# Two-block transformer kernel: gate units ahead of the attention, second half by token halves and single heads, 28 gather buffers

## The chip, the cores and the metric

The kernel runs on one core of one Trainium2 chip. The metric is the device time of one execution in microseconds (us); the kernel before takes 1839.51 us, the median of 3 runs (1837.49 to 1839.92). All data are 32-bit floats.

## The reference

`x` is 256 tokens of 1024 numbers. The first block (a convolution branch, a windowed attention, a mixture of experts) is not touched by the change, except for the order of two loads at its very start. The second block is, cut to what matters:

```python
h = modulate(rmsnorm(x, norm_mix_g), sh1, sc1)
q, k, v, z_hy, gates = split(h @ w_in)
attn = gqa_blocks(q, k, v)            # 8 heads; q and k normed and rotated; plus the context's k, v
hy = hyena(z_hy, ...)                 # short convolution, two long ones (as products of spectra)
g_attn, g_hy = split(gates)           # 1024 columns each
merged = (sigmoid(g_attn) * (attn @ w_attn_out)
          + sigmoid(g_hy) * (hy @ w_hy_out))
x = x + g1 * (merged @ w_out)
xt = modulate(rmsnorm(x, norm_ffn_g), sh2, sc2)
# peer(), in chunks of 128 tokens, 8 heads:
q = xt @ wq                           # 8 heads x 2 halves x 128
s1, s2 = q[.., 0] @ keys1.T, q[.., 1] @ keys2.T   # 128 keys each
v1, i1 = top_k(s1, 16); v2, i2 = top_k(s2, 16)
best, pos = top_k(v1[:, None] + v2[None, :], 16)  # of the 256 sums
eidx = 128 * i1[pos // 16] + i2[pos % 16]         # a row of 16384
a = einsum('chkd,cd->chk', u_tab[eidx], xt)
wgt = gelu(a) * softmax(best)
x = x + g2 * einsum('chk,chkd->cd', wgt, v_tab[eidx])
out = rmsnorm(x, final_norm_g)
```

Each token takes 8 x 16 = 128 rows of 4 KB from each of two tables. That is 512 gathers of 128 rows (512 KB each): 256 of table u, 256 of table v.

## The kernel before

It is written out by hand, engine by engine, with semaphores; program order on each engine is the order below. Feature-major tiles hold 256 tokens in columns (`actT`: 8 chunks of 128 features), token-major ones 128 tokens in the partitions (t = 0, 1). Weights come in pieces of 2 MB through the six slots of `ring`, in the order of `pieces2`; SyncE (SP) reloads a slot when the PSUM bank that last used it is full. A matrix product fills one of the eight PSUM banks; `last.then_inc(bank_full[b])` hands it to VectorE (DVE) or ScalarE (ACT), which empties it (`copy_out`, `half_out`). Nearly all matrix products are recorded on one line, L405 (`mm`), transposes on L413, L926, L942 and others.

The second block on TensorE (PE), in order:

1. the projections q and kv (token-major), then `hy0` to `hy2` (6 units of 16 products 128x256);
2. transposes of q and k; `k2_ready` is set by DVE when it has rotated q and k, done the short convolution and copied the keys;
3. the attention, 16 units of scores, softmax, transposes and products with v, with the parts of the hyena convolutions between them; it runs hand in hand with DVE and ACT;
4. `merge`: eight gate units (16 products 128x256 each) and eight output units (8 products each) in turn, each pair over all 256 tokens; `bmerged` at the end;
5. the transposes of the keys (L926), the output projections `out_unit_rows` of (t, n) = (0,0), (0,1), (1,0), the transposes of the normed tokens of t = 0, the projection (1,1);
6. `queries` (32 products 128x128 each, one per piece pq0 to pq3 and t), `key_scores` (t, g) for two heads each, and `tokens_back`, which leaves the tokens in PSUM banks 0 to 3 for the dots.

DVE then does for each group j of two heads (j = 0 to 7, t = j // 4) `picks_of(j)`: the top 16 of four lists of 128, the top 16 of two lists of 256 sums, and the rows' numbers; the last step sets `rowid_ready`. `dots_of(j)` multiplies each of the group's 32 gathered rows of u with the tokens (L2093, one instruction per row). `weigh(j)` needs the exponentials of ACT. PE sums the rows of v (`sum_rows`, L999: two products 128x512 with a diagonal matrix per row, which ACT makes on L1453); in the last two groups every other row is summed by DVE (L2124).

GpSimd (POOL) issues the 512 gathers, one after the other (L1150), group by group in the order of `TURNS`: u0, u1, v0, u2, v1, u3 and so on to v7. Gather n goes to buffer n % 24 and waits until the row of gather n - 24 has been read. The buffers are the ring's slots 1 to 4, 0 and part of 5; a buffer's first use waits for the piece of weights that held it (`slot_reader`), five first uses take spare tiles instead. The order of DVE is picks 0, picks 1, dots 0, weigh 0, then for j = 1 to 7: dots j, weigh j, picks j + 1. On ACT the copies of all key scores stand ahead of the first exponentials.

## Time and profile before

| | |
|---|---|
| median of 3 runs | 1839.51 us (1837.49 to 1839.92) |
| the profiled execution | 1844.83 us; its span 1842.8 us |
| PE, DVE, ACT, POOL busy | 81%, 48%, 16%, 27% of the span |
| chain that ended last | PE 73%, issue 9%, POOL 6%, DMA 5%, DVE 3%, an unknown queue 3% |
| HBM read | 563.5 MB, of it 268.8 MB on the queue of the gathers |

All stages below are in time from the start of the span: the first block ends near 750 us, the second block's dense part runs from there to about 1043 us, when the first gather is issued, and the gathers and sums run to the end. PE is busy nearly all the time up to 1043 us and about six tenths of it afterwards. "Issue" and "remote" as what ended an idle time mean that the profile shows nothing that the engine waited for, or a queue that it doesn't know.

### The profile page before, as it was taken

Reading aid. Unit: us, or ns where it says so; the run is one execution under the profiler, and the core shown is the slowest. Engines: PE = TensorE matmul, PEld = TensorE weight load, DVE = VectorE, ACT = ScalarE, POOL = GpSimd, SP = SyncE. Lnnn points to the kernel's source line nnn. Section 1 sums busy time; section 2 is a strip of 40 time slices with the busy share of each in tenths; the row PEclk is TensorE's granted clock in tenths of the full one; section 3 lists DMA queues with packets and bytes.
Section 4 is the critical chain, followed back from the end, with each engine's and each line's share of the span. In section 5 each row is a group of like instructions: output and inputs, shape, how many; then the busy total and the mean of one; then the engine's idle time right before and its main releaser. Section 6 shows DMA issues by size and latency. Waiting matters only on the chain.

```text
span 1842.8 us, 17400 instructions
## 1 busy us (share of the span) xinstructions
PE 1497.4 (81%) x6106; PEld 826.1 (45%) x6106; DVE 889.1 (48%) x1991; ACT 303.8 (16%) x634; POOL 501.4 (27%) x540
## 2 busy tenths in 40 slices
PE   7999989999999999889999862765858584848376
PEld 6866564443434434575786762322323231313122
DVE  3986143322223232465302774484646556564844
ACT  3113222111101111214201103020202020211001
POOL 3000000000000000000000255657574757575764
PEclk9999989999999999999999976787878786878798
DMA  9649458999999999630134488979897989898996
GB/s 320 246 143 375 163 246 342 427 428 428 429 429 428 429 429 415 223 137 1 58 114 145 148 311 315 371 273 396 303 411 293 397 303 384 301 392 301 388 374 258
DMA packets 135272, 565.35 MB, mean 307 GB/s; under 512 B 11497, under 2 KB 17430, under 8 KB 122732
## 3 DMA queue, kind: packets, MB, share of 16 engines
q1 hardware_dynamic: 60588, 295.66, 40.2%
q0 software_dynamic: 74416, 268.84, 38.3%
q8 instruction: 32, 0.52, 0.1%
q14 instruction: 28, 0.23, 0.0%
q10 hardware_dynamic: 208, 0.09, 0.0%
HBM read 563.49 MB, written 1.06 MB: 306 GB/s over the span
## 4 chain that ended last, share of the span: by engine, by line
PE 73%; issue 9%; POOL 6%; DMA 5%; DVE 3%; another core or an unknown queue 3%; ACT 1%; SPq 0%; DVEq 0%; ACTq 0%
PE psum L405 52%; PE psum L999 20%; POOL ring L1150 6%; DMA ring<-in_ada_w_dram 2%; DMA ring<-in_peer_v_dram,attnT 2%; DMA ring<-in_peer_u_dram,attnT 1%; DVE scratch L2093 1%; DMA arena<-in_hf_w_dram 1%; PE psum L413 0%; PE psum L785 0%; PE psum L791 0%; SPq L1013 0%; PE psum L860 0%; DVE ring L1961 0%
## 5 line engine op out<-in xcount | busy, mean ns | idle before, releaser
L999 PE MATMUL psum<-ring,arena 128*128 128x512 f32 x904 | 440.8, 639 | 268.8 <-DMA ring<-in_peer_v_dram,attnT 140.3
L1150 POOL DMA_INDIRECT ring<-in_peer_u_dram,attnT x251 | 236.1, 941 | 1190.4 <-DVE attnT L2067 1070.7
L999 PEld LDWEIGHTS psum<-ring,arena 128*128 128x128 f32 x904 | 182.0, 204 | 527.1 <-issue 395.7
L2093 DVE CUSTOM_DVE_ANT_0 scratch<-ring,psum 128x1024 f32<-128x1024 f32 x251 | 303.8, 1221 | 86.0 <-DMA ring<-in_peer_u_dram,attnT 57.8
L405 PE MATMUL psum<-ring,arena 128*64 128x512 f32 (+1 forms) x1552 | 343.8, 594 | 1.4 <-DVE arena L1822 1.4
L405 PE MATMUL psum<-actT,ring 128*128 128x256 f32 (+1 forms) x1424 | 269.2, 349 | 28.7 <-issue 26.9
L1150 POOL DMA_INDIRECT ring<-in_peer_v_dram,attnT x256 | 246.6, 963 | 129.3 <-issue 82.6
L405 PEld LDWEIGHTS psum<-actT,ring 128*128 128x128 f32 x1424 | 238.9, 197 | 58.0 <-issue 34.8
L405 PEld LDWEIGHTS psum<-ring,arena 128*64 128x64 f32 (+1 forms) x1552 | 110.5, 137 | 219.2 <-issue 205.8
L1864 DVE TENSOR_TENSOR arena<-arena,psum 128x512 f32<-128x512 f32 x16 | 16.9, 1058 | 203.9 <-PE psum L405 203.9
L1453 ACT ACTIVATE arena<-ident,attnT 128x128 f32<-128x128 f32 x226 | 72.8, 390 | 170.5 <-remote 67.8
L405 PEld LDWEIGHTS psum<-arena,scratch 128*128 128x128 f32 x544 | 63.3, 192 | 13.3 <-issue 13.3
L405 PE MATMUL psum<-arena,scratch 128*128 128x128 f32 x544 | 67.8, 278 | 0.0
L405 PE MATMUL psum<-tok,arena 128*128 128x512 f32 x128 | 59.2, 605 | 0.0
L2124 DVE SCALAR_TENSOR_TENSOR scratch<-ring,attnT,scratch 128x1024 f32<-128x1024 f32 x29 | 37.2, 1284 | 43.3 <-DMA ring<-in_peer_v_dram,attnT 33.2
L405 PE MATMUL psum<-ring,tok 128*128 128x512 f32 x128 | 56.0, 595 | 1.6 <-DVE tok L1691 1.6
L1190 ACT ACTIVATE arena<-psum 128x512 f32<-128x512 f32 x38 | 22.7, 597 | 197.4 <-PE psum L405 155.0
L1888 DVE TENSOR_TENSOR resid<-resid,psum 128x512 f32<-128x512 f32 x64 | 44.0, 688 | 13.8 <-PE psum L405 13.8
L1437 ACT ACT_TABLE_LOAD x7 | 9.0, 1283 | 250.7 <-DVE attnT L2080 250.6
L2025 DVE MAX8 qT<-arena 128x8 f32<-128x128 f32 x64 | 17.1, 288 | 66.8 <-remote 47.4
L1577 DVE SCALAR_TENSOR_TENSOR arena<-arena,colsB 128x256 f32<-128x256 f32 x120 | 47.7, 477 | 0.0
L1882 DVE COPY tok<-psum 128x512 f32<-128x512 f32 x16 | 11.1, 692 | 72.9 <-PE psum L405 72.9
(380 smaller groups left out, 1196.1 us busy)
## 6 DMA issues: line engine op xcount, KB each, us to landing
ring<-in_w_gate_dram SPq DMA_DIRECT2D x32, 2048.0 KB, 12.1
ring<-in_w_up_dram SPq DMA_DIRECT2D x32, 2048.0 KB, 16.5
ring<-in_w_down_dram SPq DMA_DIRECT2D x32, 2048.0 KB, 14.3
ring<-in_w_in_dram SPq DMA_DIRECT2D x15, 2048.0 KB, 14.9
ring<-in_ada_w_dram SPq DMA_DIRECT2D x12, 2048.0 KB, 11.7
ring<-in_w_out_dram SPq DMA_DIRECT2D x4, 2048.0 KB, 8.8
ring<-in_peer_wq_dram SPq DMA_DIRECT2D x4, 2048.0 KB, 10.5
ring<-in_w_attn_out_dram SPq DMA_DIRECT2D x2, 2048.0 KB, 8.9
```

Source lines behind the costliest of these rows:

```text
L405: return nc.tensor.matmul(o, lhsT, rhs, start=(k == 0), stop=(k == n - 1))
L999: last = nc.tensor.matmul(psum[:, 4 + 2 * t + n, :], diag[:, i, :], row_buf(b, use)[:, n * 512:(n + 1) * 512], start=first, stop=final)
L1150: pool.indirect_dma_start(out=row_buf(b, use), out_offset=None, in_=tab, in_offset=bass.IndirectOffsetOnAxis(ap=rowid[:, j // 4, k:k + 1], ...
L1190: last(nc.scalar.activation(dst, full(act, name)[:, 0:w], func, **kw), name)
L1453: nc.scalar.activation(diag[:, i, :], ident[:, :], ACT.Identity, scale=gates[:, j // 4, k:k + 1]).then_inc(ev("diag_ready"), 1)
L1577: V.scalar_tensor_tensor(yT[:, c, :], vpad[:, c, j:j + T], w, yT[:, c, :], ALU.mult, ALU.add).then_inc(ev("tap"), 1)
L1864: V.tensor_tensor(hperm, silu.rearrange("p (q k) -> p q k", k=4), psum[0:BOTH, 4, :].rearrange("p (q k) -> p q k", k=4), ALU.mult).then_in ...
L1882: V.tensor_copy(yrow[:, 512:1024], psum[0:BOTH, 6, :]).then_inc(ev("y_ready1"), 1)
L1888: V.tensor_tensor(r, r, psum[:, MIX_BANK[n, t], :], ALU.add).then_inc(ev("mixed"), 1)
L2025: v_pair(V.max(vals[:, 8 * r:8 * r + 8], src))
L2093: V.tensor_tensor_reduce(dotjunk[:, i % 2, :], row_buf(b, use), x, 1.0, 0.0, ALU.mult, ALU.add, dots[:, t, k:k + 1]).then_inc(ev("dotted"), 1)
L2124: V.scalar_tensor_tensor(acc, row_buf(b, use), w, acc, ALU.mult, ALU.add).then_inc(ev("added"), 1)
```

## The change

The weights get another order, with a slot for each piece given by hand. All eight gate units stand ahead of the attention: the four of the first branch behind the hyena projections, the four of the second behind the transposes of q and k. ACT keeps their sigmoids, the first four in `mergedT`, the second four over `actT`. After the attention the output units are done by token halves (`mixed_half`, 16 products 128x128), the merge by token halves (`merge_half`), and the norm, queries and key scores of t = 0 start while t = 1 is unfinished. The queries and key scores of group 0, and its picks, are done by single heads; `rowid_ready` is set once for each. There are 28 row buffers, filled by a table `ROW_ORDER` up to gather 53 and after that by which was read the longest ago; eight dots of group 0 are done between the steps of t = 1. The second output gate row, the keys and the final gain have other places in memory. At the start, the piece `wg` is issued behind four small loads. Some semaphores are shared by name.

```diff
-ROWBUFS = 24
+ROWBUFS = 28
...
+        rowbufs = [dft[:, :, :, :].rearrange("p a t c -> p (a t c)"), idft[:, :, :].rearrange("p a t -> p (a t)")]
+        rowbufs += [ring[:, 3, r * D:(r + 1) * D] for r in range(4)] + [ring[:, 4, r * D:(r + 1) * D] for r in range(4)]
+        rowbufs += [tok2[:, 0, :], tok2[:, 1, :]]
+        rowbufs += [ring[:, s_, r * D:(r + 1) * D] for s_ in (2, 5, 1, 0) for r in range(4)]
...
+        ROW_ORDER = [*range(10), *range(4), 10, 11, *range(4, 8), *range(12, 20), *range(8, 12), *range(0, 6), *range(20, 24), *range(6, 10), *range(12, 16), *range(24, 28)]
...
-            pe.wait_ge(ev("qk2_ready"), 1)
+            gate_units2(0)
+            pe.wait_ge(ev("proj_ready"), 1)
...
+            gate_units2(1, (4, 5, 6, 7))
             emptied(pe, "qT0")
             emptied(pe, "qT1")
-            pe.wait_ge(ev("k2_ready"), 1)
+            pe.wait_ge(ev("proj_ready"), 3)
...
-            merge(place2, "b", [(attnT, tuple(f"pw{i}" for i in range(4))), (hyoT, ())])
+            def mixed_half(br, t, u):
+
+                wo = ring[:, place2[f"o{br}"][0], :].rearrange("p (k n) -> p k n", k=KC)
+                b = bank(f"bo{br}{t}{u}")
+                for c in range(4):
+                    m = (4 * u + c) * P
+                    for k in range(KC):
+                        last = mm(psum[:, b, c * P:(c + 1) * P], wo[:, k, m:m + P], (attnT, hyoT)[br][:, k, t * P:(t + 1) * P], k, KC)
+                last.then_inc(bank_full[b], 1)
...
+            room_reader = {2: "bo011", 6: "bo111", 10: "bx11", 12: "pq01", 16: "pq11", 20: "pq21", 24: "pq31"}
...
+                    if table == "u" and (i == 0 or (j == 0 and i == PTOP)):
+                        pool.wait_ge(ev("rowid_ready"), j + 2 if j else 1 + (i > 0))
+                    if use == 1 and b in room_reader:
+                        full(pool, room_reader[b])
+                    if use > 1:
+                        reader, count = row_reader(before_)
                         pool.wait_ge(ev(reader), count)
...
-            picks_of(0)
+            best_of(0, (0,), "0a")
+            rows_of_table(0, (0,))
+            merge_half(1, 1, 1)
+            best_of(0, (1,), "0b")
+            rows_of_table(0, (1,))
+            shift_of(0)
+            mix_in(1, 0)
+            dots_of(0, range(0, 4), 1)
+            mix_in(1, 1)
+            dots_of(0, range(4, 5), 1)
+            pn_rows(1)
+            dots_of(0, range(5, 8), 1)
+            half_out("pn", 1, modsc[:, 2, :], mod[:, 24:32, 0])
             picks_of(1)
-            dots_of(0)
+            dots_of(0, range(8, GROUP))
```

The order on PE from the hyena projections (the first row) to the first scores, before:

```order
L405 MATMUL psum<-actT,ring 128x256 x96
L839 MATMUL psum<-ident,arena 128x128 x8
L844 MATMUL psum<-ident,arena 128x128 x2
L405 MATMUL psum<-kdup,qT 128x512 x4
L883 MATMUL psum<-ident,arena 128x128 x8
```

and in the changed program:

```order
L404 MATMUL psum<-actT,ring 128x256 x160
L822 MATMUL psum<-ident,arena 128x128 x8
L827 MATMUL psum<-ident,arena 128x128 x2
L404 MATMUL psum<-actT,ring 128x256 x64
L404 MATMUL psum<-kdup,qT 128x512 x4
L867 MATMUL psum<-ident,arena 128x128 x8
```

64 products of the gates now stand ahead of the transposes of q and k, and 64 between these and the scores (`kdup,qT`).

PE again, from the last of the eight pairs of gate and output units to the second group's scores (`ring,tok` are the output projections, `actT,ring` 128x128 the queries, `spec,arena` the key scores), before:

```order
L405 MATMUL psum<-actT,ring 128x256 x16
L405 MATMUL psum<-arena,ring 128x256 x8
L926 MATMUL psum<-ident,ring 128x128 x16
L405 MATMUL psum<-ring,tok 128x512 x24
L413 MATMUL psum<-ident,scratch 128x128 x8
L405 MATMUL psum<-ring,tok 128x512 x8
L405 MATMUL psum<-actT,ring 128x128 x32
L413 MATMUL psum<-ident,scratch 128x128 x8
L405 MATMUL psum<-spec,arena 128x128 x4
L405 MATMUL psum<-actT,ring 128x128 x32
```

and in the changed program, from the third and fourth half of the output units on:

```order
L404 MATMUL psum<-arena,ring 128x128 x32
L404 MATMUL psum<-attnT,ring 128x128 x16
L404 MATMUL psum<-ring,tok 128x512 x16
L404 MATMUL psum<-attnT,ring 128x128 x16
L932 MATMUL psum<-ident,arena 128x128 x16
L412 MATMUL psum<-ident,scratch 128x128 x8
L404 MATMUL psum<-arena,ring 128x128 x16
L404 MATMUL psum<-actT,ring 128x128 x16
L944 MATMUL psum<-ident,actT 128x128 x8
L404 MATMUL psum<-spec,arena 128x128 x2
L404 MATMUL psum<-actT,ring 128x128 x16
L404 MATMUL psum<-arena,ring 128x128 x16
```

Two of the four output projections, three of the four halves of t = 1 and half of the first queries are ahead of the first key scores; the other two projections come later.

DVE, from the end of the second head's picks to the second group's (L2009 and L2010 add an output projection, L2105 is a dot, L2015 and L2016 the norm, L1524 the modulation), in the changed program; before, L2003 to L1524 of t = 1 stood ahead of all picks, and the dots behind the second group's:

```order
L2092 TENSOR_TENSOR attnT<-kdup 128x32
L2009 TENSOR_TENSOR scratch<-spec,psum 128x512
L2010 TENSOR_TENSOR resid<-resid,scratch 128x512
L2105 ISA scratch,attnT<-dft,psum 128x1024
L2105 ISA attnT 128x1
L2105 ISA scratch,attnT<-idft,psum 128x1024
...
L2009 TENSOR_TENSOR scratch<-spec,psum 128x512
L2010 TENSOR_TENSOR resid<-resid,scratch 128x512
L2105 ISA scratch,attnT<-ring,psum 128x1024
...
L2015 RECIPROCAL st<-st 128x1
L2016 TENSOR_SCALAR scratch<-resid,st 128x1024
```

The steps that free t = 1 for PE's later queries now stand behind the picks of both heads and between eight dots.

## Rows read from the trace of the kernel before

**Rows 1.** Windows: busy time per engine, granted clock, DMA share.
```profile
core 0: us, PE busy (x) PEld busy (x) DVE busy (x) ACT busy (x) POOL busy (x), PEclk, DMA share, GB/s
900.00:1000.00 100.00, 100.00 (x455) 83.77 (x454) 12.22 (x18) 9.25 (x15) 0.00 (x0) 1.00 0.34 118
...
1100.00:1150.00 50.00, 13.82 (x94) 13.23 (x94) 23.96 (x45) 17.87 (x44) 29.13 (x31) 0.60 0.83 323
```

**Rows 2.** Timeline of PE, around the attention: start, length, line, idle before.
```profile
774.86 41.60 PE L405 MATMUL psum<-actT,ring 128*128 128x256 f32 x192
...
822.68 3.69 PE L405 MATMUL psum<-kdup,qT 64*128 64x512 f32 x8 [5.13 <-DVE st L1944]
...
905.11 7.07 PE L405 MATMUL psum<-actT,ring 128*128 128x256 f32 x32
912.01 3.62 PE L405 MATMUL psum<-attnT,ring 128*128 128x256 f32 x16
```

**Rows 3.** Timeline of PE: projections, queries, the last key scores.
```profile
989.75 20.87 PE L405 MATMUL psum<-ring,tok 128*128 128x512 f32 x48
...
1018.20 7.31 PE L405 MATMUL psum<-actT,ring 128*128 128x128 f32 x64
...
1037.64 12.56 PE L405 MATMUL psum<-actT,ring 128*128 128x128 f32 x111
...
1108.23 0.37 PE L405 MATMUL psum<-actT,ring 128*128 128x128 f32 x1 [1.74 <-issue]
...
1119.76 4.63 PE L405 MATMUL psum<-spec,arena 128*128 128x128 f32 x40
```

**Rows 4.** Timeline of DVE: picks, dots and waits.
```profile
1028.76 0.49 DVE L2025 MAX8 qT<-arena 128x8 f32<-128x128 f32 x2 [0.91 <-ACT arena L1190]
...
1042.87 0.18 DVE L2067 CAST attnT<-attnT 128x32 int32<-128x32 f32 x1
...
1058.18 1.22 DVE L2093 CUSTOM_DVE_ANT_0 scratch<-ring,psum 128x1024 f32<-128x1024 f32 x1
...
1128.24 0.19 DVE L2104 TENSOR_REDUCE st<-attnT 128x2 f32<-128x32 f32 x1 [23.20 <-ACT attnT L1437]
...
1183.01 0.15 DVE L2098 COPY st<-epscol 128x1 f32<-128x1 f32 x1 [2.37 <-remote]
...
1293.36 0.76 DVE L2040 TENSOR_TENSOR spec<-qT 128x256 f32<-128x256 f32 x2 [3.90 <-remote]
```

**Rows 5.** Timeline of POOL: gathers 0, 1, 21, 41, 96 and 175.
```profile
1043.33 1.03 POOL L1150 DMA_INDIRECT ring<-in_peer_u_dram,attnT  x1 [1028.49 <-DVE attnT L2067]
1044.67 0.97 POOL L1150 DMA_INDIRECT ring<-in_peer_u_dram,attnT  x1 [0.30 <-issue]
...
1084.07 0.94 POOL L1150 DMA_INDIRECT ring<-in_peer_u_dram,attnT  x1 [10.55 <-PE psum L405]
...
1120.20 0.94 POOL L1150 DMA_INDIRECT ring<-in_peer_u_dram,attnT  x1 [11.54 <-PE psum L405]
...
1209.21 0.94 POOL L1150 DMA_INDIRECT ring<-in_peer_u_dram,attnT  x1 [11.74 <-DVE attnT L2067]
...
1325.57 0.94 POOL L1150 DMA_INDIRECT ring<-in_peer_u_dram,attnT  x1 [3.13 <-PE psum L999]
```

**Rows 6.** Windows within the gathers, and one whole period.
```profile
1285.00:1290.00 5.00, 1.52 (x2) 0.49 (x2) 1.02 (x5) 0.00 (x0) 1.89 (x3) 0.70 1.03 409
...
1295.00:1300.00 5.00, 4.63 (x6) 1.95 (x6) 4.59 (x22) 0.00 (x0) 2.81 (x3) 0.50 0.48 143
...
1325.00:1330.00 5.00, 5.00 (x13) 2.09 (x11) 4.85 (x9) 2.66 (x8) 3.52 (x4) 1.00 0.92 311
...
1304.07:1400.76 96.69, 65.10 (x138) 27.43 (x137) 56.10 (x133) 13.14 (x36) 60.12 (x64) 0.82 0.91 347
```

**Rows 7.** The page's DMA queues, one row.
```profile
q8 instruction: 32, 0.52, 0.1%
```

**Rows 8.** Timeline of PE at the start of the kernel.
```profile
20.81 0.31 PE L475 MATMUL psum<-ident,kdup 100*128 100x100 f32 x1 [1.15 <-DMA arena<-in_hf_w_dram]
```

More of the change, by code:

```diff
@@ L1 @@
 from contextlib import ExitStack
+import collections
 import itertools
@@ L917, in _ @@
             hy_back(1, 1)
[L918 to L922 removed]
+            def mixed_half(br, t, u):
[5 more added lines that the diff above has]
+                        last = mm(psum[:, b, c * P:(c + 1) * P], wo[:, k, m:m + P], (attnT, hyoT)[br][:, k, t * P:(t + 1) * P], k, KC)
+                last.then_inc(bank_full[b], 1)
+            landed(place2, "o0")
+            for i in range(4):
+                emptied(pe, f"pw{i}")
+            mixed_half(0, 0, 0)
+            mixed_half(0, 0, 1)
+            landed(place2, "o1")
+            pe.wait_ge(ev("hy_ready"), 1)
+            mixed_half(1, 0, 0)
+            mixed_half(1, 0, 1)
+            mixed_half(0, 1, 0)
+            pe.wait_ge(ev("bmerged"), 1)
+            out_unit_rows(place2, "b", 0, 0)
+            out_unit_rows(place2, "b", 0, 1)
+            mixed_half(0, 1, 1)
+            pe.wait_ge(ev("keys_in"), 32)
+            kp = arena1[:, 0:2048].rearrange("p (c d) -> p c d", d=P)
             for g in range(4):
@@ L1359, in _ @@
                 last(nc.scalar.activation(hpad[:, j % 2, :, 1:T + 1], ps, ACT.Copy), f"hy{j // 2}{j % 2}")
+            for i in range(4):
+                copy_out(f"bg0{i}", pair(mergedT, i), func=ACT.Sigmoid)
             for g in range(2):
-                copy_out(f"qT{g}", qT[:, 2 * g:2 * g + 2, :].rearrange("p c t -> p (c t)"))
+                copy_out(f"qT{g}", pair(qT, g))
+            full(act, "bg13")
+            for i in range(4):
+                copy_out(f"bg1{i}", pair(actT, i), func=ACT.Sigmoid)
             def exp_unit(u):
@@ L1376, in hy_spectrum @@
             def hy_spectrum(o, part):
-                if o == 0 and part == 0:
-                    act.wait_ge(ev("y_ready1"), n_iter)
                 for f in range(NT):
@@ L1996, in _, with merge_half @@
             hy_gate(1, 1)
-            merge("b")
+            def merge_half(br, t, u):
+                cs, ts = slice(4 * u, 4 * u + 4), slice(t * P, (t + 1) * P)
+                dst = mergedT[:, cs, ts]
+                ps = full(dve, f"bo{br}{t}{u}").rearrange("p (c t) -> p c t", c=4)
+                if br == 0:
+                    last(V.tensor_tensor(dst, dst, ps, ALU.mult), f"bo{br}{t}{u}")
+                else:
+                    m = mtmp["b"][:, u, :].rearrange("p (c t) -> p c t", c=4)
+                    last(V.tensor_tensor(m, actT[:, cs, ts], ps, ALU.mult), f"bo{br}{t}{u}")
+                    v(V.tensor_tensor(dst, dst, m, ALU.add), "bmerged" if u else None)
+            for br in range(2):
+                for i in range(4):
+                    emptied(dve, f"bg{br}{i}")
+            for br in range(2):
+                for u in range(2):
+                    merge_half(br, 0, u)
+            merge_half(0, 1, 0)
             dve.wait_ge(ev("g1_in"), 16)
```

336 lines of the change are left out of this document (147 added, 189 removed).

## Prediction, made before the changed kernel ran

> **What bounds the kernel now.** I read the windows first: busy time of each engine and DMA share. Ahead of the first gather TensorE is at 100 us of 100 between 900 and 1000 with DMA share 0.34, so there the end is set by PE's products [rows 1]; within the gathers PE is at 13.8 of 50 us in one stretch [rows 1] and at 65 of 96.7 us in a whole period, at DMA share 0.91 [rows 6], so there the transfers and the waits between them set it. The timelines of PE, DVE and POOL then give the steps. PE's row of the attention is preceded by 5.13 us of waiting for DVE [rows 2]. Pairs of a gate unit (7.07) and an output unit (3.62) follow [rows 2]; then projections, 20.87 for three, and queries of t = 0 [rows 3]. DVE's picks start at 1028.76 and its last cast is at 1042.87 [rows 4]; the first gather starts at 1043.33, and the next stands 1.34 later, 0.97 busy and 0.30 between [rows 5]. From then on both ends pull: POOL waits 10.55 and 11.54 us for PE's late queries to free weights' slots [rows 5], while PE itself stands at "issue" (1.74 before one product) and DVE waits 23.20 for ACT's exponentials, which stand behind all copies of the key scores [rows 3, 4]. The third group's u gathers start at 1209.21, after 11.74 of waiting for row numbers [rows 5]. After that the kernel is periodic: 64 gathers (one u and one v group) in 96.69 us [rows 6].
>
> **Where the steady period goes.** A gather is 512 KB; at 409 GB/s, the rate in the stretch at DMA share 1.03 [rows 6], it takes 1.28 us, so 64 take 82 us. The other 15 are two waits. DVE's next picks crawl while the DMA engines are full and get on only when these drain: share 0.48 at 1295 to 1300, with a step of the picks at 1293.36 after 3.90 us of "remote" [rows 4, 6]. And in the u part POOL waits 3.13 us for a buffer that PE has to empty [rows 5], through which DMA keeps going at a share of 0.92 [rows 6], a loss of (1.03 - 0.92) x 5 = 0.6 us in that window and about 1.2 us over the whole wait. My reading of the crawl, on PE and DVE alike, is that their own instructions arrive late: the queue of instructions moved 0.52 MB in 32 packets, 16 KB each [rows 7], through the engines that the gathers fill.
>
> The Trainium skill, "Runtime: NRT & Kernel Launch", section "Instruction fetch mechanics", says that each sequencer fetches 16 KiB blocks by its own DMA queue and that the cost of crossing into a new one is mostly hidden. The packets' size agrees with [rows 7]; "hidden" does not agree with the waits of 1.74 and 3.90 us in [rows 3, 4], if these are such crossings. By the page's rule PE wouldn't be starved; that is rival B below.
>
> **The change, part by part.** The profiled execution has a span of 1842.8 and took 1844.8; the median is 5.3 below that. I sum on the span and carry the difference over.
>
> *Start.* PE waits 1.15 us for a small load at 20.81 [rows 8]; with `wg` behind the small loads this goes, but wg's own product may be late: between -2 (worse) and +1.15. I take +1.
>
> *Gates first.* Eight units of 6.91 (the hyena row has six in 41.60, so 6.93 [rows 2]) move from behind to ahead of the attention: 55.4 us, nothing saved in PE. What they cover: the 5.13 us wait for DVE [rows 2] lies under the second four. But ACT now does four sigmoids between PE's last gate unit and the attention, which bounds this from 0 to the old 5.13; I take a new wait of about the same lag, 4 us, less 2 to 3 hidden. The attention shifts by +52.5 (822.7 to 875.2) and ends near 957.8; the gates are then missing behind it.
>
> *From the attention to the first head's scores.* PE, in order: five output halves of 3.6 (a whole unit, 3.62, is 8 products of 256 columns; a half, 16 products of 128 columns, costs like half a query row of 7.31 [rows 3]: 3.6) = 18; two projections of 6.95 (20.87 / 3 [rows 3]) = 13.9; one half, 3.6; 16 transposes of the keys and 8 of the tokens, 1.9 and 1.0 (at the queries' 7.31 / 64 = 0.114 each [rows 3]); one half, 3.6; half the queries, 3.6; tokens back 1.0, the same way; two scores and their copies, 1.8 by my estimate from short steps of 0.2 to 0.9 [rows 4]. Sum 48.4, so the first picks start near 957.8 + 48 = 1006, against 1028.76 [rows 4]: 23 earlier. The halves have half as many columns each, so double the weight loads; these lie under the products as in [rows 1], where loads take 83.8 us of a full 100.
>
> *Picks of one head.* Both heads took 1042.87 - 1028.76 = 14.1 us [rows 4]. One head is between 7.1 (all by elements) and 14.3 (all fixed cost); the rows are short instructions (0.49 for one list of 128), so nearer to half: 8.7. First gather at 1014.5, 29 us ahead of 1043.33.
>
> *What the second head and t = 1 pay.* `merge_half(1,1,1)` on DVE now stands behind the first head's picks, and `mix_in` of t = 1 behind both heads' with eight dots in between; behind them PE's projections of t = 1, the norm, the transposes and PE's queries of t = 1 wait. I get the projections at 1016 to 1030, the queries of t = 1 at 1042.5, 5 us later than 1037.64 [rows 3]. That order is a price: 5 us of the 29.
>
> *The slots of weights.* POOL's first 28 rows have buffers that come free early or by dots (ten free tiles, then the eight early dots). From gather 28 on it waits for products of PE again, as at 1084.07 and 1120.20 [rows 5], and then for the dots of group 1. So the 29 us are worth only what PE's last queries and DVE's second dots give.
>
> *PE's last queries.* From 1037.64 to the last scores' end at 1124.4 [rows 3] are 86.8 us, for some 51 us of products; 36 are waits at "issue". The gathers now start 29 us earlier and PE's queries 5 later, so PE has about 51 us of work from 1042.5, and is done at 1093.5 if never starved, or at 1093.5 + 36 = 1129.5 if starved as before. POOL is held up from 1041 to 1058 by slots, during which DMA isn't full; some 40 to 45 us of the work see full DMA. With the old ratio (36 lost on some 62 us) these lose 23 to 26. Then ACT's exponentials and DVE: dots of group 1 start near 1120 (between 1098 and 1133), against 1130 (the 23.20 wait ended at 1128.24 [rows 4]).
>
> *To the third group.* Dots of group 1 started near 1130.3, after the small steps behind 1128.24, and their end is 1183.01 [rows 4]: 52.7 us where 32 instructions of 1.14 (1.22 long [rows 4], overlapping by 0.08) are 36.8; from their end to u2 it was 26.2 [rows 4, 5]. So u2 is 63 to 79 us behind the start of the dots. I take 63: 36 gathers left after the dots begin are 46 us of transfer, and behind them about 17 us of drain and picks; the 16 us of starving fell into the old, later queue of gathers. u2 at 1183 against 1209.21: 26 gained, of the 29.
>
> *28 buffers.* Six periods follow. With four more buffers the 3.13 us wait [rows 5] goes. It costs DMA 1.2 us each time: 6 x 1.2 = 7 to 8. Bounds: 0, as picks still end some 10 us after the drain whatever POOL does, and 6 x 3.3 = 20, if all of each wait counts.
>
> Sum: 1 + 26 + 8 = 35. 1839.5 - 35 = **1804**; by the span, 1808.
>
> **Rivals.**
> *A, the above*: with u2 between 1175 and 1195 and the buffers at 0 to 12, 1790 to 1818.
> *B, PE isn't starved in the first groups.* Its waits have shares of ACT's and DVE's emptying in them, and single heads break those up. Dots of group 1 start at 1098, u2 at 1161, 48 earlier; with 6 x 2 us of the buffers and the start, about 60: 1779. It speaks against this that the 1.74 wait has no releaser in the profile [rows 3].
> *C, the change doesn't do what it says*: the early rows are fetched and then stand. All starving remains, the last queries end at 1129.5, group 1's dots start at 1130, and the gathers from 60 on wait for these as before. Left are fewer rows to move behind the dots, 63 to 70 instead of 79, and the buffers: 15 to 23, so about 1820. For it: the waits for PE's slots ended the same [rows 5].
> *D, slower.* With POOL never waiting for a buffer, the DMA engines stay full through each u group, and the block of DVE's instructions that now comes in during a 3 us gap falls into the dots, as in group 1: 16 us there. The place is each of the six later periods, the price up to 9 us each (16, less the 7 that the dots are early), 54 in all, set against the gain of 35: 1858. It decides from 35 / 6 = 6 us a period on. Against it: the dots of the later groups stand at full DMA already, and DVE is busy 4.85 of 5 us at share 0.92 [rows 6].
>
> **How the numbers follow.** A 0.55, B 0.15, C 0.20, D with its full price 0.06, and 0.04 for D near its deciding point. About 0.2% (3.7 us) is what a measurement of this kernel can tell from no change. A, B and C are all faster: 0.90; within 0.2%: 0.04; slower: 0.06. The time is A's, 1804. The range takes in B's centre with 3 us beyond it, C to 1820 and its slow side by half the unknown cost: 1776 to 1829; outside are D and the edge of B.
>
> **What would show it.** Right: the attention's first scores near 875, first picks near 1006, first gather near 1014, queries of t = 1 near 1042, group 1's dots near 1120, gather 96 near 1183, periods of 95 to 96 with no waits of 3 us for buffers, no wait of 1.15 at the start. Each is a term of the sum and can be read alone. B is shown by dots of group 1 before 1105 without "issue" waits on PE; C by their start at 1130 in spite of a first gather at 1014; D by periods above 100. It would be wrong altogether if the first picks came later than 1020, for instance by ACT's sigmoids holding up the attention by 10 us or more, or if `mix_in` of t = 1 behind the picks put PE's last queries past 1060.

## The result and the profile after

The changed kernel takes 1846.90 us, the median of 20 runs (1842.21 to 1854.44), and the kernel before, in 20 runs beside it, 1842.83 us (1837.49 to 1847.25): ratio 1.0025, interval 1.0013 to 1.0036. It is slower by a quarter of a per cent, where 1804 was forecast; the range ended at 1829. The profiled execution of the changed kernel has a span of 1840.4 us, at the lower end of its runs, and that of the kernel before one of 1842.8 in the upper half of its own. So the two traces differ by -2.4 us where the medians differ by +4.1; that gap of 6.5 is spread between runs. Most of it lies ahead of the gathers: in the 17 undisturbed traces of this and the later kernels whose code up to there is the changed kernel's, the first gather starts between 1010.1 and 1019.6. Behind gather 96 traces of one kernel differ less: two of one kernel below take 619.5 and 619.2 us from there to the end.

The gathers are numbered from 0 in the order in which they are issued; a period is 64 of them, one group of rows of u and one of v. POOL's gathers 0, 20, 96, 160 and 224 in the changed kernel (start, length, idle before and what ended it):

```profile
1013.81 1.03 POOL L1154 DMA_INDIRECT dft<-in_peer_u_dram,attnT  x1 [998.97 <-DVE attnT L2075]
...
1057.95 0.95 POOL L1154 DMA_INDIRECT ring<-in_peer_u_dram,attnT  x1 [17.66 <-PE psum L404]
...
1195.76 0.94 POOL L1154 DMA_INDIRECT ring<-in_peer_u_dram,attnT  x1 [16.24 <-DVE attnT L2075]
...
1291.84 0.94 POOL L1154 DMA_INDIRECT ring<-in_peer_u_dram,attnT  x1 [11.99 <-DVE attnT L2075]
...
1390.68 0.94 POOL L1154 DMA_INDIRECT ring<-in_peer_u_dram,attnT  x1 [15.57 <-DVE attnT L2075]
```

| | before | forecast | after |
|---|---|---|---|
| attention's first scores | 822.68 | 875 | 875.33 |
| first picks | 1028.76 | 1006 | 1004.67 |
| first gather | 1043.33 | 1014.5 | 1013.81 |
| queries of t = 1 begin | 1037.64 | 1042.5 | 1048.62 |
| last key scores end | 1124.4 | 1116 to 1120 | 1121.6 |
| dots of group 1 begin | 1130.3 | 1120 | 1127.5 |
| gather 96 | 1209.21 | 1183 | 1195.76 |
| five periods, gathers 96 to 416 | 480.6 | 474 to 475 | 492.8 |
| gather 416 to the end | 153.0 | 152 | 151.9 |

The dense part came out within 2 us up to the first gather, closer than the spread of some ten us between traces gives reason to expect, and the first gather is 29.5 us earlier. Of these, 13.4 are left at gather 96, and the five periods behind it give 12.2 of those back: 96.1, 98.8, 98.8, 100.2 and 98.9 us, against 94.9, 96.7, 96.1, 97.0 and 96.0. The rows of a period's end show what is new. Windows of 4 us at the end of a v group, before (the same columns as [rows 1], the last three being the granted clock, the DMA share and GB/s):

```profile
1384.00:1388.00 4.00, 1.01 (x1) 0.57 (x2) 0.65 (x3) 0.00 (x0) 0.94 (x1) 0.50 1.01 399
1388.00:1392.00 4.00, 3.36 (x4) 1.13 (x4) 1.83 (x8) 0.00 (x0) 1.07 (x2) 0.50 0.06 25
1392.00:1396.00 4.00, 4.00 (x10) 1.69 (x9) 3.86 (x19) 0.00 (x0) 1.74 (x2) 0.89 0.83 240
1396.00:1400.00 4.00, 4.00 (x11) 1.85 (x10) 3.98 (x10) 0.00 (x0) 0.00 (x0) 1.00 0.39 154
```

and after, behind one row for the whole period and two windows from within it:

```profile
1291.84:1390.68 98.84, 63.30 (x129) 26.46 (x128) 55.87 (x133) 13.24 (x36) 60.33 (x65) 0.78 0.90 350
1303.84:1307.84 4.00, 4.00 (x11) 1.82 (x10) 3.84 (x7) 0.40 (x1) 2.99 (x4) 1.00 1.03 410
1355.84:1359.84 4.00, 4.00 (x11) 1.72 (x10) 0.66 (x3) 0.00 (x0) 3.09 (x4) 1.00 1.03 410
1375.84:1379.84 4.00, 1.50 (x2) 0.57 (x2) 0.76 (x2) 0.00 (x0) 0.00 (x0) 0.50 1.03 410
1379.84:1383.84 4.00, 2.54 (x3) 0.91 (x3) 2.37 (x10) 0.00 (x0) 0.00 (x0) 0.50 0.25 99
1383.84:1387.84 4.00, 4.00 (x7) 1.64 (x6) 3.86 (x15) 0.00 (x0) 0.00 (x0) 0.65 0.00 0
1387.84:1391.84 4.00, 4.00 (x11) 1.81 (x10) 2.62 (x7) 1.13 (x1) 0.94 (x1) 1.00 0.00 0
```

In both, DVE gets through 0.65 to 0.76 us of its picks in 4 us while the DMA share is 1.0, and 3.86 some 4 us after it has fallen. This is what I call the crawl. It isn't POOL that holds DVE up: at 1375.84 POOL does nothing and DVE has 0.76 all the same. Nor does every instruction crawl: at the same share of 1.03, DVE's dots have 3.84 of 4 us (1303.84), and PE is busy all 4 us beside crawling picks (1355.84). Before, the engines ran empty (0.06) while three of the 32 gathers of the v group were still to be issued; these then ran beside the rest of the picks (0.83, 0.39). After, all gathers of the group have been issued by then, and during the last 8 us of the picks nothing is transferred. What held the gathers back before is in POOL's rows of the kernel before, gathers 220, 221 and 224. By the program the first two can only wait for a buffer, which PE's sums have to empty, though the profile names no releaser; the third waits for row numbers:

```profile
1384.31 0.94 POOL L1150 DMA_INDIRECT ring<-in_peer_v_dram,attnT  x1 [3.05 <-issue]
...
1390.62 0.94 POOL L1150 DMA_INDIRECT ring<-in_peer_v_dram,attnT  x1 [5.37 <-remote]
...
1400.76 0.93 POOL L1150 DMA_INDIRECT ring<-in_peer_u_dram,attnT  x1 [6.71 <-DVE attnT L2067]
```

3.05 + 5.37 us are in the v group, 6.71 at its end, 15.1 in all; after, it is 15.57 at the end alone. POOL waits as long in both; what differs is how much is left to transfer when DVE gets going. In the prediction I had looked at the buffer wait of the u group [rows 5] and not at this pair.

### The profile page after: what moved, and what is told of

It reads as the page before. It is cut to its first block, busy times and chain, and to the rows that moved or that the text cites. A ratio compares the mean times of both kernels' runs of the same rounds, so it can differ in the third digit from the quotient of the medians.

```text
span 1840.4 us, 17693 instructions
## 1 busy us (share of the span) xinstructions
PE 1502.5 (82%) x6234; PEld 833.8 (45%) x6234; DVE 890.8 (48%) x2004; ACT 304.2 (17%) x637; POOL 503.1 (27%) x540
## 4 chain that ended last, share of the span: by engine, by line
PE 67%; issue 10%; POOL 9%; DVE 5%; DMA 5%; another core or an unknown queue 2%; ACT 1%; SPq 0%; POOLq 0%; DVEq 0%; ACTq 0%
PE psum L404 52%; PE psum L1011 14%; POOL ring L1154 8%; DMA ring<-in_ada_w_dram 2%; DVE scratch L2105 2%; DMA ring<-in_peer_v_dram,attnT 1%; DMA dft<-in_peer_v_dram,attnT 1%; POOL tok L1154 1%; DMA ring<-in_w_in_dram 1%; PE psum L412 0%; PE psum L755 0%; PE psum L761 0%; DMA ring<-in_peer_u_dram,attnT 0%; DVE attnT L2105 0%
## 5 line engine op out<-in xcount | busy, mean ns | idle before, releaser
L1011 PE MATMUL psum<-ring,arena 128*128 128x512 f32 x772 | 380.3, 644 | 228.3 <-DMA ring<-in_peer_v_dram,attnT 122.4
L1011 PEld LDWEIGHTS psum<-ring,arena 128*128 128x128 f32 x772 | 155.9, 205 | 449.5 <-issue 335.7
L2105 DVE CUSTOM_DVE_ANT_0 scratch<-ring,psum 128x1024 f32<-128x1024 f32 x216 | 260.5, 1220 | 67.2 <-DMA ring<-in_peer_u_dram,attnT 35.6
L1154 POOL DMA_INDIRECT dft<-in_peer_u_dram,attnT x10 | 9.5, 953 | 1002.1 <-DVE attnT L2075 999.0
L1154 POOL DMA_INDIRECT ring<-in_peer_u_dram,attnT x216 | 204.3, 946 | 219.0 <-DVE attnT L2075 92.0
L1154 POOL DMA_INDIRECT ring<-in_peer_v_dram,attnT x218 | 210.8, 967 | 76.2 <-issue 66.5
L2138 DVE SCALAR_TENSOR_TENSOR scratch<-ring,attnT,scratch 128x1024 f32<-128x1024 f32 x24 | 30.8, 1285 | 39.2 <-DMA ring<-in_peer_v_dram,attnT 39.2
L1011 PE MATMUL psum<-dft,arena 128*128 128x512 f32 x40 | 22.0, 662 | 31.7 <-DMA dft<-in_peer_v_dram,attnT 25.3
```

The costliest lines, as they stand in the source:

```text
L1011: last = nc.tensor.matmul(psum[:, 4 + 2 * t + n, :], diag[:, i, :], rowbufs[b][:, n * 512:(n + 1) * 512], start=first, stop=final)
L1154: pool.indirect_dma_start(out=rowbufs[b], out_offset=None, in_=tab, in_offset=bass.IndirectOffsetOnAxis(ap=rowid[:, j // 4, k:k + 1], axis ...
L2105: V.tensor_tensor_reduce(dotjunk[:, i % junk, :], rowbufs[b], x, 1.0, 0.0, ALU.mult, ALU.add, dots[:, t, k:k + 1]).then_inc(ev("dotted"), 1)
L2138: V.scalar_tensor_tensor(acc, rowbufs[b], w, acc, ALU.mult, ALU.add).then_inc(ev("added"), 1)
```

## The experiments

The kernels were run in sets, each with runs of the kernel before among them, and each ratio is to those. The times came at two levels, whatever the kernel: in some sets the kernel before took 1837 to 1843 us (medians), as above; in others 1729 to 1730 us (level B below; the first is level A). All kernels of one set share its level. Each set behind the result ran on a chip of its own: A came on chips 11 and 1, B on chips 8, 4, 10 and 12. So the level may belong to the chip, but no chip was used twice, and the chip of the result above isn't on record. Why there are two is not shown by the profile; what differs is shown below, and it served as an experiment of its own.

One measure is used throughout: the time from gather 96 to the end, in the profiled executions. At level A it is 633.6 us before and 644.6 in the changed kernel.

**24 buffers in the steady part.** From gather 96 on only 24 of the 28 are used; all ahead of that is the changed kernel.

```diff
-            b = ROW_ORDER[n] if n < len(ROW_ORDER) else min(last_use, key=last_use.get)
+            b = ROW_ORDER[n] if n < len(ROW_ORDER) else min((x for x in last_use if n < 96 or x < 24), key=last_use.get)
```

> The changed kernel, but from gather 96 on (the third u group) only 24 of its 28 row buffers are used; everything ahead of that is as in the changed kernel. Theory 1 (the four more buffers lengthen the steady period: they take away POOL's waits in the v groups, 3.1 and 5.4 us before gathers 220 and 221, in which the DMA engines ran empty while DVE's picks caught up and three gathers were still left to run beside the rest of the picks): gather 96 stays at 1196, the five periods after it go from 98.5 back to about 96.2 us, total about 12 us below the changed kernel, 1835, ratio to before 0.996. Rival 2 (the longer periods come from the places and the order of reuse of the buffers, or from where the instructions of DVE and PE fall): the periods stay at 98 to 99, ratio 1.002.

Level A: 1829.31 us, ratio 0.9925 (0.9897 to 0.9953). That is 1.0% under the changed kernel's ratio of 1.0025, or some 18 us by comparison across sets; 12 were expected. Its trace is of an execution of 2110 us, where the other six took 1821 to 1836, so the periods themselves can't be read at level A. Three repeats came at level B.

> The kernel with 24 of the 28 buffers from gather 96 on once more, for an undisturbed trace. The first theory (28 buffers lengthen the period): gather 96 near 1195, waits for a buffer near the end of each v group, 5 to 8 us of waiting for row numbers at its end instead of 15.6, the five periods after gather 96 sum to 475 to 482 instead of 492.8, total 1822 to 1835. The rival (places and order): they sum to 490 or more.

> 24 of the 28 buffers from gather 96 on. Where engines crawl: ratio 0.990 to 0.996, the five periods after gather 96 sum to 475 to 483 instead of 492.8, with waits for buffers late in the v groups and under 8 us of wait for row numbers. Where they don't crawl: nothing to be won, ratio 0.990 to 0.994 like the changed kernel's 0.9914 there.

> 24 of the 28 buffers from gather 96 on. Where engines crawl: ratio 0.990 to 0.996, the five periods after gather 96 sum to 475 to 483 instead of 492.8, with waits for buffers late in the v groups and under 8 us of wait for row numbers. Where they don't crawl: 0.991 as before.

At level B it took 1714.93, ratio 0.9919 (0.9892 to 0.9946); an earlier set gave 1713.32, ratio 0.9910 (0.9891 to 0.9929), and one single run 1716.37. The changed kernel itself has 0.9914 there (below). So four buffers fewer gain a per cent at level A and nothing that can be told at B: what the 28 cost exists only at level A.

**Holding gathers back.** 28 buffers, and POOL waits ahead of the last four, or the last sixteen, gathers of v0 to v5 until DVE has finished the lists of the group whose row numbers are next.

```diff
+                    if table == "v" and 0 <= j <= LAST - 2 and i == 28:      # the second kernel: i == 16
+                        pool.wait_ge(ev("stage_ready"), 2 + j + 2)
...
                 v_done()
+                if len(heads) == 2:
+                    v(V.tensor_copy(stat("dummy", 1), epscol[:, 0:1]), "stage_ready")
                 sums = [
```

> The changed kernel with 28 buffers, but POOL holds back the last four gathers of each v group (v0 to v5) until DVE has the top lists of the group whose row numbers come next. This puts an empty stretch of the DMA engines where the 24 buffers had one, without taking buffers away. Theory 1: rows are transferred beside the tail of the picks again; periods of 95 to 97 instead of 98.5, total 1831 to 1837, ratio 0.995. Rival 2 (places and order of the buffers): periods stay at 98 or grow by the wait, ratio 1.002 or more.

> As the kernel that holds back four gathers, but the last sixteen of each v group are held back until DVE has the top lists. Theory 1, carried further (DVE crawls through the lists only while the DMA engines are full, and runs at its own speed once they have run empty): the lists are done some 5 us after the engines run empty, sixteen gathers (20 us) then run beside about 11 us of picks, and the wait for row numbers at the end of the group goes; periods of 88 to 91, total about 1800, ratio 0.975. Rival 3 (DVE crawls again as soon as gathers run, whatever its start): the picks' tail takes 30 us instead of 11, periods of 100 or more, ratio over 1.005.

Level A, four held back: 1829.11, ratio 0.9904 (0.9873 to 0.9935); the five periods sum to 477.9, and from gather 96 to the end it is 634.7. Buffers, places and order are those of the changed kernel with its 644.6, so the rival that puts the longer periods down to places and order falls. Sixteen held back: 1821.40, ratio 0.9870 (0.9835 to 0.9905); the five periods sum to 465.2, 93.0 each instead of 98.6. Two POOL rows of each, the first gather behind the hold and the first of the next u group:

```profile
1379.29 1.00 POOL L1156 DMA_INDIRECT ring<-in_peer_v_dram,attnT  x1 [5.71 <-DVE st L2046]
...
1390.70 0.95 POOL L1156 DMA_INDIRECT ring<-in_peer_u_dram,attnT  x1 [6.68 <-DVE attnT L2079]
```

```profile
1367.89 1.00 POOL L1156 DMA_INDIRECT ring<-in_peer_v_dram,attnT  x1 [5.53 <-DVE st L2046]
...
1388.01 0.95 POOL L1156 DMA_INDIRECT ring<-in_peer_u_dram,attnT  x1 [0.30 <-issue]
```

With four held back, the waits are nearly those of the kernel before (5.71 and 6.68, against 5.37 and 6.71). With sixteen, the wait for row numbers is gone (0.30), at the price of 5.53 in the middle. The rival here was that DVE would crawl again as soon as gathers run; the windows of that period speak against it:

```profile
1367.89:1372.00 4.11, 4.11 (x11) 1.82 (x10) 4.11 (x18) 0.00 (x0) 3.19 (x4) 1.00 0.57 152
1372.00:1380.00 8.00, 8.00 (x20) 3.50 (x19) 5.29 (x15) 2.28 (x5) 6.17 (x7) 1.00 0.93 325
```

DVE is busy 4.11 of 4.11 us; its picks end at 1377.4, some 10 us after the release, at full speed beside gathers. The DMA share in these windows is 0.57 and 0.93, not the 1.03 of the crawl, so they don't show what picks do at a full one. I expected periods of 88 to 91 and they are 93, and a total of 1800 that came out at 1821: the u groups have a wait of 5.95 us of their own now (gather 115: "remote"). Both kernels beat the kernel before and the changed one at level A. The one with sixteen was run once more:

> 28 buffers, the last sixteen gathers of v0 to v5 held back until DVE has the top lists. Where engines crawl: 0.987 as before. Where they don't (before near 1730): DVE has the lists some 6 us after the dots of the group, which the dense stretch of gathers puts near the 12th v gather; by the theory that holding pays only by ending the crawl, POOL waits 0 to 3 us for them, nothing is gained, and the ratio is between the changed kernel's 0.991 and 0.998.

It came at level A again: 1816.74, ratio 0.9896 (0.9879 to 0.9912), with before at 1837.02; its five periods sum to 465.4. What it does at level B was not measured.

**Slower v gathers.** POOL does a memset behind each v gather and waits for it; its step goes from 1.244 to 1.32 us. (For a form without that wait there is no time.)

```diff
+                    if table == "v":
+                        nc.gpsimd.memset(stat("pace", 1), 0.0).then_inc(ev("pool_set"), 1)
+                        pool.wait_ge(ev("pool_set"), 2 + paced)
```

> The changed kernel, with a memset of 128x1 on POOL behind each gather of a v group, which it waits for: its step there goes from 1.244 to 1.4 us or more, slower than the 1.28 us of a transfer. Theory (instructions come late because the DMA engines are never without a gather): DVE's picks run at their own speed beside the v gathers, the wait for row numbers goes from 15.6 to 5 us or less, against 3 to 6 us of slower gathers: periods of 88 to 94 instead of 98.5, ratio to before 0.985. Rival (the crawl isn't tied to full engines): periods 3 to 6 us longer, ratio 1.012.

The repeats:

> The changed kernel with POOL's step in the v groups slowed by a waited-for memset to about 1.34 us. Where engines crawl (before near 1843): if they crawl because a gather is always queued, periods go from 98.5 to 88 to 94, ratio 0.985; if the crawl isn't tied to that, periods 3 to 6 us longer, ratio 1.012. Where they don't crawl: periods of 83, ratio 0.994 as before.

> The changed kernel with POOL's step in the v groups slowed by a waited-for memset to about 1.34 us. Where engines crawl (before near 1843): if they crawl because a gather is always queued, periods go from 98.5 to 88 to 94, ratio 0.985; if the crawl isn't tied to that, periods 3 to 6 us longer than the changed kernel's, ratio 1.012. Where they don't crawl: 0.994 as before.

> The changed kernel with POOL's step in the v groups slowed by a waited-for memset to about 1.34 us. Where engines crawl (before near 1840): if they crawl because a gather is always queued, DVE's picks run at their own speed, the wait for row numbers of 15.6 us goes to 5 or less, periods from 98.5 to 88 to 94, ratio 0.985; if the crawl isn't tied to that, periods 3 to 6 us longer than the changed kernel's, ratio 1.012. Where they don't crawl: 0.994 as before.

All four sets with it came at level B: 1720.57, 1718.89, 1718.71 and 1720.74 us, ratios 0.9938 (0.9921 to 0.9955), 0.9941, 0.9939 and 0.9941, 0.25% above the changed kernel there. A window about as long as one period of it:

```profile
1231.00:1315.00 84.00, 54.71 (x121) 23.83 (x120) 54.32 (x133) 14.20 (x34) 63.95 (x97) 0.82 1.03 409
```

No crawl was there to be cured, and it cost 2.0 us a period (415.4 to 415.9 in five, against 405.7), near the 2.4 of 32 slower steps. Nor did it do what it was for: the DMA share stayed at 1.03, and the mean of POOL's steps in u and v groups, 1.28 us, is just the length of a transfer. What it would do at level A stays open. So does

> The changed kernel with 16 more instructions on DVE ahead of the lists of groups 1 to 7, each a copy of one column (0.15 us). Where engines crawl: if the crawl is a price per instruction (0.7 us each while gathers fill the DMA engines), the lists end up to 11 us later in each period, or, as the rest of the picks waits for the engines to run empty anyway, about the 11 us of instructions that then move behind it at their own 0.2 us: 2 to 4 us a period, ratio 1.006 to 1.02. If the crawl is waiting for other engines' data: under 0.5 us a period, ratio 1.002. Where they don't crawl: 0.991 to 0.993.

for which the 16 copies stood ahead of the lists (`for q in range(16): V.tensor_copy(more[:, q:q + 1], epscol[:, 0:1])`). Level B: 1714.51, ratio 0.9913 (0.9891 to 0.9936), the same as without them. What 16 more instructions cost where there is a crawl was thus not tested. That the crawl isn't one price for each instruction is seen without them, in the windows of the dots and of PE at share 1.03 above.

**The two kernels without the crawl.**

> The changed kernel itself beside the kernel before. Two kinds of chip have shown up: in one, engines crawl at one instruction per 0.7 us or a multiple of it while gathers run (before at 1839 to 1847), in the other they don't (before at 1727 to 1732). If this is the first kind: ratio 1.001 to 1.004, periods of 98 to 99. If it is the second: nothing is lost in the periods (80 to 83 each, set by POOL and the transfers), the dense part's gain stays, and the ratio is 0.990 to 0.995.

> The kernel before itself, for a trace of it beside the others. Where engines don't crawl (time near 1730): no issue waits on PE between 1037 and 1090, periods of 80 to 84, gather 96 near 1165. Where they do (near 1843): as its first trace, gather 96 near 1209, periods of 95 to 97.

Level B: the changed kernel 1715.17, before 1729.97, ratio 0.9914 (0.9888 to 0.9939); it is faster by 0.9%. The traces (spans 1716.6 and 1729.5), one period of each, first the changed kernel and then before:

```profile
1233.07:1313.18 80.11, 50.53 (x112) 22.11 (x111) 54.27 (x133) 12.99 (x31) 60.59 (x65) 0.81 1.03 410
1290.00:1300.00 10.00, 10.00 (x18) 4.13 (x18) 9.76 (x54) 0.07 (x1) 7.54 (x9) 0.75 1.02 408
```

```profile
1247.01:1328.93 81.92, 56.63 (x129) 24.78 (x128) 54.59 (x133) 14.75 (x36) 60.70 (x64) 0.85 1.03 409
```

In the second row DVE does its picks: 9.76 of 10 us busy at DMA share 1.02 and 408 GB/s. At level A the same code at the same share had 0.76 of 4. So full DMA engines alone do not make the engines crawl, against what I had read from [rows 6].

The first gather starts at 1017.72 after and 1044.70 before, 27.0 earlier, and gather 96 at 1153.25 and 1165.61, 12.4 earlier. At level A the same two numbers are 29.5 and 13.4: between them 14.6 us are lost at B and 16.1 at A, so this loss doesn't need the crawl.

The five periods sum to 405.7 and 412.6, but what 28 buffers gain there is gone at the end: from gather 416 on the changed kernel takes 157.6 us against 151.3. The kernel with 24 of the 28 buffers settles that both come from the buffers. Its three traces at level B have 412.3 to 412.6 in the five periods and 151.2 to 151.3 behind them. Gather 416 in the changed kernel (span 1716.6) and with 24 buffers (span 1709.9):

```profile
1558.98 0.94 POOL L1154 DMA_INDIRECT ring<-in_peer_u_dram,attnT  x1 [0.30 <-issue]
...
1558.74 0.94 POOL L1154 DMA_INDIRECT ring<-in_peer_u_dram,attnT  x1 [0.30 <-issue]
```

From gather 96 to the end it is 563.9 us before, 563.4 with 28 buffers and 563.7 to 563.8 with 24. The periods count issues, and with more buffers POOL issues further ahead of transfers that go no faster (409 and 410 GB/s); that is my reading of why both differ and their sum doesn't.

PE in the dense part at level A, the changed kernel:

```profile
1028.88 3.73 PE L404 MATMUL psum<-actT,ring 128*128 128x128 f32 x32
...
1043.26 2.05 PE L404 MATMUL psum<-spec,arena 128*128 128x128 f32 x8 [10.65 <-issue]
...
1048.62 9.06 PE L404 MATMUL psum<-actT,ring 128*128 128x128 f32 x64 [1.61 <-ACT actT L1190]
...
1117.00 4.63 PE L404 MATMUL psum<-spec,arena 128*128 128x128 f32 x40
```

and at level B:

```profile
1032.78 3.73 PE L404 MATMUL psum<-actT,ring 128*128 128x128 f32 x32
...
1038.32 1.13 PE L404 MATMUL psum<-spec,arena 128*128 128x128 f32 x8 [1.81 <-issue]
...
1044.30 9.79 PE L404 MATMUL psum<-actT,ring 128*128 128x128 f32 x64 [3.98 <-issue]
...
1091.42 4.63 PE L404 MATMUL psum<-spec,arena 128*128 128x128 f32 x40
```

From the queries of t = 1 to the last scores it is 73.0 us at A and 51.8 at B; from the end of the queries ahead of the scores to those of t = 1 it is 16.0 and 7.8. In the 10.65 us PE waits for a copy by ACT, which stands still itself:

```profile
1033.92 0.29 ACT L1401 ACTIVATE st<-st,epscol 128x1 f32<-128x1 f32 x1
1042.78 0.38 ACT L1194 ACTIVATE arena<-psum 128x256 f32<-128x256 f32 x1 [8.56 <-remote]
```

The queries it copies were done at 1032.6. At level B the same copy follows at once:

```profile
1037.84 0.38 ACT L1194 ACTIVATE arena<-psum 128x256 f32<-128x256 f32 x1
```

So ACT stands still too at level A, some 20 us after the first gather. That the gathers cause it is my reading; the two kernels meant to test it, next, met only level B.

**The gathers and PE's last queries.** Two edits of POOL's waits, one for each kernel.

```diff
-            room_reader = {2: "bo011", 6: "bo111", 10: "bx11", 12: "pq01", 16: "pq11", 20: "pq21", 24: "pq31"}
+            room_reader = {2: "bo011", 6: "bo111", 10: "bx11", 12: "pq31", 16: "pq31", 20: "pq31", 24: "pq31"}
```

```diff
+                    if turn == 0 and i == 8:
+                        full(pool, "pq01")
```

> The changed kernel, but gathers 20 and on wait for PE's last query bank, where they waited for the bank of the queries that had used their slot. No gather runs beside PE's queries of t = 1 and after. Theory (PE's issue waits of 1 to 2.4 us in that stretch are its own instructions, late because of the gathers): the queries from 1048.6 on take 51 us instead of 73, dots of group 1 can start near 1107 instead of 1127, but 76 gathers (97 us) are left from 1098 on, so gather 96 comes at 1200 to 1210 against 1195.8: ratio to before 0.999 to 1.008. Rival (PE's waits there have another cause, as banks that ACT empties late): the queries still take 65 us or more, and gather 96 comes at 1220 or later, ratio over 1.012.

> The changed kernel, but gather 8 and on wait for the bank of the first queries of t = 1: only the eight rows of the early dots are fetched ahead of those queries. Theory (ACT's standstill from 1034.2 to 1042.8, which held PE up for 10.65 us, is the gathers' doing): that wait is under 2 us, the queries of t = 1 start near 1039 instead of 1048.6, and their first bank is full near 1046; gather 96 within 6 us of 1195.8, ratio 1.000 to 1.004. Rival (ACT waits for something in the new order of the work itself): the 10 us stay, the twelve gathers come 13 us later for nothing, gather 96 at 1205 or later, ratio over 1.006.

> The changed kernel with gather 20 and on held until PE's last query bank. Where engines crawl: the queries take 51 us instead of 73 if the gathers are their hindrance, dots of group 1 start near 1110, gather 96 at 1200 to 1212, ratio 1.000 to 1.010; if the gathers aren't the hindrance, 65 us or more and ratio over 1.012. Where they don't crawl: 1.011 as before.

> The changed kernel with gather 8 and on held until the first query bank of t = 1. Where engines crawl: PE's wait of 10.65 us ahead of the second group's scores goes to 2 us (it was 1.82 where they don't crawl), the queries of t = 1 start 8 to 9 us earlier, gather 96 comes within 6 us of 1195.8, ratio 1.000 to 1.004; if that wait is ACT's for another reason, it stays and the ratio is over 1.006. Where they don't crawl: 0.998 as before.

Both were run in two sets, all at level B. Held until the last query bank: 1746.65 and 1748.27, ratios 1.0108 (1.0086 to 1.0130) and 1.0103. Held after eight: 1724.88 and 1726.09, ratios 0.9984 (0.9966 to 1.0003) and 0.9979 (0.9966 to 0.9992). Their expectations on PE's crawl could not be put to the test there; PE's wait ahead of the second group's scores was 1.8 us in all of them. What they show at level B is the worth of the early gathers without a crawl: the first puts gather 20 at 1089.6 instead of 1054.4 and costs 1.9%, some 33 us; the second puts gather 8 some 22 to 25 us later, but gather 20 only 10 to 15 later, and costs 0.7%, 11 us. Of each us by which gather 20 comes later, three quarters or more are lost at the end, by these single traces.

## Why the prediction was wrong

The sum was 1 + 26 + 8 = 35 us. In the two traces it is 0 at the start, 13.4 at gather 96, -12.2 in five periods and +1.1 behind them, 2.4 us; the medians have -4.1. Two steps failed: the 28 buffers, by 20 us, and what is left at gather 96, by 13.

*Gates first, halves, single heads.* Right in size: the attention's shift by 52.7 us (52.5 forecast), first picks at 1004.67 (1006), first gather at 1013.81 (1014.5). The waits inside the shift were others than I took: no wait for ACT's sigmoids ahead of the scores, where I had 4 us, and 2.04 for DVE ahead of the second four gates, in place of the old 5.13. That they came out equal, and that this trace lies in the middle of the spread of 1010 to 1020, is luck. Having the gates ahead of the attention, the work of t = 1 behind the first picks, and single heads gained 29.5 us there.

*Start.* Taken at +1. No wait for the load is left near 20 us, but the hyena projections start at 775.16 against 774.86 [rows 2]: worth nothing.

*What t = 1 pays.* Forecast 5 us, measured 11 (1048.62 against 1037.64). What failed here is that I put the crawl only on PE's queries. At level B the start is 7.8 us behind the last of the earlier queries, which at level A would be 1040.4; ACT's standstill of 8.56 made it 1048.6.

*PE's last queries.* 73.0 us, against 51 + 23 to 26 forecast. Right in size; with the later start and ACT's exponentials, dots of group 1 began 7.5 us behind the forecast.

*To the third group.* 68.3 us from the first of those dots to gather 96, against 63: another 5. So the failed step in its own terms: I forecast that group 1's dots start 10 us earlier than before and that u2 follows them 16 us closer, 26 in all; measured are 2.8 and 10.6, 13.4 in all. The waits above are where these us went at level A, but they are not shown to be the reason: at level B, without them, gather 96 is only 12.4 us earlier. What limits it there was not tested. Gather 20 gives a hint: it is 16.0 us earlier at B and 14.6 at A, held up in both by one of PE's slots (10.41 and 17.66 us), and of that only 3.6 and 1.2 us are lost by gather 96. This much rival C had: most of the early rows' gain is given back.

*28 buffers.* The failed term: +8 forecast, -12.2 measured. I bounded it at 0 from below, "as picks still end some 10 us after the drain whatever POOL does". That is true, and it is the reason for the loss: what POOL still has to issue at the drain runs beside these 10 us, and with 28 buffers that is nothing. A wait that I had priced as a pure loss was the moment at which DVE got going. Where there is no crawl, at level B, the term isn't +8 either: the periods are 1.4 us shorter each, against the 1.2 that I took, but the end takes it back (563.4 us from gather 96 on, 563.9 before).

*Rival D* had the cause (no wait for a buffer, so no gap in which the instructions come in) but the wrong place, the dots of the u groups, and 9 us a period where 2.4 were measured. Its deciding point, 6 us a period, was worked out against a gain of 35; against 13.4, over the five periods measured, the point is 2.7. I gave it 0.10 with its milder form. *Rival B* had PE without starving, which exists, but took the kernel before as crawling all the same: both lose it together, and the ratio then is 0.991. Nor did gather 96 then come 48 us earlier, but 12.4.

*The cause of the crawl* stays open. The traces show that in some stretches with gathers at level A PE and DVE go on in steps near 0.7 us or multiples of it (waits of 1.05, 1.75, 2.44 us with "issue" or "remote"), that DVE's picks stop doing so within some us when the DMA engines run empty, and that the same program at the same 409 GB/s doesn't at level B. The queue of instructions has the same 33 packets at both levels. Late instructions would fit waits without a releaser, but 33 packets for an execution of 17693 instructions are far too few for one fetch per step of 0.7 us, and dots, and sums for stretches, run at full speed at the same DMA share. So the reading that I gave in the prediction is not shown, and these numbers speak against its simplest form. The Trainium skill, "Runtime: NRT & Kernel Launch", section "Instruction fetch mechanics", calls the cost of crossing into a new block mostly hidden: level B agrees (DVE busy 9.76 of 10 us), and level A, if late instructions are what it shows, doesn't.

## What to carry to other kernels

A wait on a loaded resource may be doing a service: before removing a stall, look what else gets going in it, here DVE's picks in POOL's 8 us. And a stage measured by when its work is issued can look faster without being so: take the time to the end, as the 6.9 us of 28 buffers at level B show. When two engines hand work round in a ring, place the empty stretch where most transfers are left to cover what follows; holding sixteen gathers back until the lists were ready gave 1.0 to 1.3% against the kernel before at level A, where four more buffers had made the period 2.5% longer (98.6 against 96.1 us). And an early start is worth only what the next limit lets through: of 27 to 30 us at the first gather, 12 to 13 were left 96 gathers later, at either level.

## What the runs showed of the hardware

The same kernels ran at two levels, 1836 to 1847 and 1726 to 1732 us for the kernel before, by sets and not by kernels; sets at different levels were on different chips. The mean granted clock of the changed kernel is 0.901 at A and 0.932 at B. Up to the first gather the traces agree within some us (gather 0 of the changed kernel at 1013.81 and 1017.72); the whole difference is in the part with gathers, 826.6 us at A and 698.9 at B. At level A DVE's picks and PE's queries stand still for 0.4 to 2.5 us, at times longer, before single instructions while the DMA share is 1.02 to 1.03; at level B at 1.02 they don't. At level A too, DVE's dots, and PE's sums in some stretches, run at full speed at 1.03. The sign of a change's effect can differ between the two: 1.0025 and 0.9914 for this one.
